# An encoder layer with 64 routed experts: experts' columns in units of 32 with groups of one size, and experts' weights laid out in runs of 16 KB and 8 KB a partition

## The reference, cut to what matters

```
scores = sigmoid(x @ w_router);  the 6 best of 64 experts a token (in 4 of 8 groups)
w = scores[chosen] / sum * 2.5
h_e = silu(x @ w_e_gate[e]) * (x @ w_e_up[e])      # 1024 -> 256
y   = sum over chosen e of w * (h_e @ w_e_down[e]) # 256 -> 1024
x   = LN(alpha * x + y + shared_expert(x))
```

## Time and profile before

| | |
|---|---|
| median of 3 runs | 1903.97 us (1901.08 to 1904.21) |
| the profiled execution's own time | 1900.44 us |
| its span | 1898.6 us |
| mean granted TensorE clock | 0.988 |
| PE busy | 1816.5 us, 96% |
| PE weight loads busy | 954.7 us, 50% |
| DVE / ACT / POOL busy | 655.2 / 322.4 / 148.0 us |
| DMA | 330.67 MB in 124958 packets, mean 174 GB/s |

### The profile page before, as it was taken

One profiled execution on the slowest core, in us unless ns is written; L12 is line 12 of the kernel. 1 busy time (PEld: TensorE's weight loads), 2 busy tenths in 40 slices (PEclk: granted clock), 3 DMA queues, 4 the chain that ended last, 5 costly groups with the idle time before them and its releaser, 6 DMA issues.

```text
span 1898.6 us, 18081 instructions
## 1 busy us (share of the span) xinstructions
PE 1816.5 (96%) x6817; PEld 954.7 (50%) x6817; DVE 655.2 (35%) x1008; ACT 322.4 (17%) x471; POOL 148.0 (8%) x159
## 2 busy tenths in 40 slices
PE   6999999999999999999999987999999999999976
PEld 3444456666666565556555544344444444444422
DVE  5011038888898863001115685000000000000019
ACT  1111121111111111111001210222222222222210
POOL 0000000000000000000000004111111111111112
PEclk9999999999999999999999999999999999999988
DMA  5115011110111001111162008999999999999547
GB/s 215 45 44 191 8 33 34 34 33 22 33 33 33 1 21 46 55 33 56 50 223 87 34 1 325 367 413 390 385 381 363 398 353 376 389 379 360 212 195 316
DMA packets 124958, 330.67 MB, mean 174 GB/s; under 512 B 11840, under 2 KB 68192, under 8 KB 106720
## 3 DMA queue, kind: packets, MB, share of 16 engines
q1 hardware_dynamic: 109200, 292.06, 40.9%
q0 software_dynamic: 15696, 37.77, 5.0%
HBM read 311.44 MB, written 37.75 MB: 184 GB/s over the span
## 4 chain that ended last, share of the span: by engine, by line
PE 87%; DVE 9%; DMA 1%; issue 1%; ACT 1%; DVEq 0%; SPq 0%; POOLq 0%; POOL 0%; ACTq 0%
PE pA L1020 19%; PE pg L667 10%; PE pB L1046 10%; PE pg L694 9%; PE pg L817 9%; PE pB L848 4%; PE pg L1007 3%; PE pB L895 2%; PE pA L895 2%; PE pA L840 2%; PE pg L707 2%; PE pB L750 2%; PE pX L908 1%; PE pA L787 1%; PE pA L750 1%
## 5 line engine op out<-in xcount | busy, mean ns | idle before, releaser
L694 PE MATMUL pg<-rA,hw 128*128 128x384 f32 x768 | 259.6, 486 | 0.7 <-ACT aTr L1154 0.7
L1735 DVE TENSOR_TENSOR rows<-rows,pA 128x256 f32<-128x256 f32 x53 | 22.3, 421 | 603.8 <-ACT rows L1266 603.8
L667 PE MATMUL pg<-rEF,rA 128*128 128x512 f32 x448 | 195.3, 598 | 3.1 <-ACT rCD L1133 3.1
L694 PEld LDWEIGHTS pg<-rA,hw 128*128 128x128 f32 x768 | 140.6, 190 | 84.1 <-ACT aTr L1154 0.9
L817 PE MATMUL pg<-rA,hw 128*128 128x384 f32 x512 | 165.3, 486 | 0.0
L1020 PE MATMUL pA<-rCD,aTr 128*64 128x512 f32 (+1 forms) x416 | 155.4, 594 | 0.0
L667 PEld LDWEIGHTS pg<-rEF,rA 128*128 128x128 f32 x448 | 85.8, 192 | 109.9 <-issue 109.9
L817 PEld LDWEIGHTS pg<-rA,hw 128*128 128x128 f32 x512 | 97.2, 190 | 67.6
L1020 PE MATMUL pA<-ew,aTr 128*64 128x512 f32 (+1 forms) x256 | 113.9, 598 | 0.0
L1020 PE MATMUL pA<-rEF,aTr 128*64 128x512 f32 (+1 forms) x256 | 113.2, 595 | 0.0
L1020 PE MATMUL pA<-rA,aTr 128*64 128x512 f32 (+1 forms) x240 | 106.8, 598 | 0.0
(11 more groups left out here) (304 smaller groups left out, 2387.3 us busy)
## 6 DMA issues: line engine op xcount, KB each, us to landing
rCD<-w_e_gate SPq DMA_DIRECT2D x22, 1024.0 KB, 8.7
rCD<-w_e_up SPq DMA_DIRECT2D x22, 1024.0 KB, 11.9
rCD<-w_e_down SPq DMA_DIRECT2D x22, 1024.0 KB, 12.8
hw<-w_in SPq DMA_DIRECT2D x40, 512.0 KB, 4.0
rA<-w_e_gate SPq DMA_DIRECT2D x11, 1024.0 KB, 5.4
rA<-w_e_up SPq DMA_DIRECT2D x11, 1024.0 KB, 7.5
rA<-w_e_down SPq DMA_DIRECT2D x11, 1024.0 KB, 12.5
ew<-w_e_gate SPq DMA_DIRECT2D x11, 1024.0 KB, 7.6
```

The lines of the kernel that those rows point to most:

```text
L667: last = mm(big_bank(fill), x1T[:, c, i * P:(i + 1) * P], strip[n % 2][:, c, :], start=(c == 0), stop=(c == KC - 1))
L694: last = mm(pg[:, n * 512:n * 512 + HALF], hw3[m][:, c, :], x1T[:, c, n * HALF:(n + 1) * HALF], start=(c == 0), stop=(c == KC - 1))
```

## The change

`rooms()` gives rank 0 one unit, ranks 1 to 10 four, ranks 11 to 42 three and the rest two: 179 units in place of 212, 45 rounds in place of 53, 46 blocks with the overflow's in place of 54. `pieces()` cuts all of a round in one size: 128 if one expert fills it, 64 if all borders are even, else 32, so that an expert with 96 columns in a round is three pieces of 32. Worked out from the code, the 45 rounds are 3 of one piece, 17 of two, 24 of four and a last one of three pieces of 32. On the host, gate and up are joined and laid out as (expert, 128 partitions, 4096 elements), one run of 16 KB a partition, and down as (expert, 128, 2048), one of 8 KB. SP issues two loads an expert in place of three. The layout in SBUF is the same.

```diff
 def rooms():
-    return [2] + [4] * 42 + [2] * 21
+    return [1] + [4] * 10 + [3] * 32 + [2] * 21

 def pieces(t):
-    out = []
+    spans = []
     for j in range(E):
         a = max(STARTS[j], t * UNITS) - t * UNITS
         z = min(STARTS[j + 1], (t + 1) * UNITS) - t * UNITS
-        while a < z:
-            n = 4 if a == 0 and z == 4 else 2 if a % 2 == 0 and z - a >= 2 else 1
-            out.append((j, a * UNIT, n * UNIT))
-            a += n
-    return out
+        if a < z:
+            spans.append((j, a, z))
+    whole = [z for _, _, z in spans] == [UNITS]
+    step = UNITS if whole else 2 if all(a % 2 == z % 2 == 0 for _, a, z in spans) else 1
+    return [(j, o * UNIT, step * UNIT) for j, a, z in spans for o in range(a, z, step)]
...
+        down_rows = [w[:, 4 * D:6 * D] for w in weights]
...
-            wg_d = d["w_e_gate"].rearrange("e (p c) n -> e p c n", c=KC)
-            wu_d = d["w_e_up"].rearrange("e (p c) n -> e p c n", c=KC)
-            wd_d = d["w_e_down"].rearrange("e (j p) n -> e p j n", p=P)
             def load_gate_up(e, n):
-                for m, src in ((0, wg_d), (1, wu_d)):
-                    sp.dma_start(slabs(gate_up[n][:, m * 2 * D:(m + 1) * 2 * D], KC),
-                                 src[bass.ds(e, 1), :, :, :].rearrange("e p c n -> (e p) c n")).then_inc(s_wgu[n], 16)
+                sp.dma_start(gate_up[n], d["w_e_gate_up"][bass.ds(e, 1), :, :].rearrange("e p n -> (e p) n")).then_inc(s_wgu[n], 16)
             def load_down(e, n):
-                sp.dma_start(wd[n], wd_d[bass.ds(e, 1), :, :, :].rearrange("e p j n -> (e p) j n")).then_inc(s_wd[n], 16)
+                sp.dma_start(down_rows[n], d["w_e_down"][bass.ds(e, 1), :, :].rearrange("e p n -> (e p) n")).then_inc(s_wd[n], 16)
...
-                    pe.wait_ge(s_wgu[j % NB], 32 * (j // NB + 1))
+                    pe.wait_ge(s_wgu[j % NB], 16 * (j // NB + 1))
...
-                pe.wait_ge(s_wgu[more], r * 32 + 32 * (used + 1))
+                pe.wait_ge(s_wgu[more], r * 16 + 16 * (used + 1))
...
+    gate, up, down = (arrays.pop(name) for name in ("w_e_gate", "w_e_up", "w_e_down"))
+    arrays["w_e_gate_up"] = np.concatenate([w.reshape(E, P, KC * F) for w in (gate, up)], axis=2)
+    arrays["w_e_down"] = np.ascontiguousarray(down.reshape(E, 2, P, D).transpose(0, 2, 1, 3)).reshape(E, P, 2 * D)
```

## The result

The changed kernel takes 1839.91 us (median of 4 runs, 1839.25 to 1843.92) against 1904.09 for the kernel before on the same chip: a ratio of 0.9669, 95% interval 0.965 to 0.9688, 64 us less. I forecast 1827 in a range of 1808 to 1855. A second set gave 1842.20 against 1903.75, ratio 0.968 (0.9667 to 0.9693). The profiled execution is the slowest of the first four, 1843.92 with a span of 1841.7; before it was 1900.44 and 1898.6.

What follows compares the result with a forecast made beforehand. DMA was to bound the expert stage: weights landing at 8.5 + 526.5 - 6.5 = 528.5 us plus 14 gave 542.5 against 619.7, 77 less; minus 2.5 for the first gather, net 75. Forecast 1827 us, range 1808 to 1855.

Steps and rivals of the forecast that it cites:

- PE's floor: Expert rounds: least time PE needs for the 45 rounds with fill and drain, 533 us.
- the price of a quad: Rounds of four 32-column pieces: 0.1 us a round over a pair, 2.4 us in all.
- The upper bound of 0.016 us a step: Quad rounds: issuing four load and matmul pairs takes at most 0.445 us against 0.43, 9 us in all.
- The rival in which groups of 32 take turns: Quad rounds: every step lasts 0.86 us in place of 0.43, 248 us more on PE, 2061; chance 0.05.
- the layout: Weight loads: larger blocks save 4.6 us on down and 2 on gate and up, together 6.5 us.
- The rival of a lower sustained rate: Expert stage: DMA sustains only 384 GB/s, so the gain is 35 us and the kernel takes 1866; chance 0.12.
- slow 16 KB blocks: Gate and up loads: 0.76 us a packet costs 64 us of DMA, 1891, or up to 2065; chance 0.03.
- the step from the bytes to the last weights' landing: Expert stage: 218.5 MB at 415 GB/s, 526.5 us, plus 8.5, less 6.5, land 528.5 us after the first up.
- 542.5: Expert stage, first up to end: last landing at 528.5 us plus 14 behind it, against 619.7 before.
- the clock at nothing: PE after DMA stalls: three or four might cost 1.7 us each, which DMA makes up; priced at nothing.
- the first gather: Start of the rounds: the gather stands behind larger preload blocks, 2.5 us later; later gathers hide.
- The rivals' 1816, 1866 and 2061: Whole-kernel times if PE stays the bound (chance 0.16), DMA sustains less (0.12), or groups take turns (0.05).

Runs made afterwards that it cites:

- the reordered kernels: Changed kernel with experts of 64 columns moved to the order's end: five 1832.75 us, eight 1827.40, eight with gathers first 1826.68, eight with 8 KB gate/up blocks 1832.37.
- f1: Changed kernel with SP waiting for the first two gathers to land before preloading the fifth and sixth expert: 1839.64 us, 0.9664 of the kernel before.
- e1: Changed kernel with its new rooms and pieces but the old weight layout (8 and 4 KB runs, three loads an expert): 1845.46 us, 0.9698 of the kernel before.
- e2: Kernel before with only the new weight layout (16 and 8 KB runs), old rooms and 53 rounds: 1904.98 us, 1.0013 of the kernel before.

## Why the prediction was right or wrong

**Right: the direction, the range and the bound.** DMA became the bound, at a mean share of 1.01 for 350 us. Landings take over 20 us. PE's floor was 533 us in the prediction; 532.3 was measured once DMA was lightened. The waits came in the later rounds, 17.0 us for my 5 to 15.

**Right: the price of a quad.** I took 0.1 us a round; it is none (7.00 for 7.02). The upper bound of 0.016 us a step from the rate of the transposes didn't bind: steps come 0.43 us apart, eight instructions in each. The rival in which groups of 32 take turns is out. The Trainium skill's some 4 ns per further tile ("TensorE: Matmul & The Clock Gate", Part 3) agrees with this trace in that a step's pieces start within 0.02 us; the 8 ns a step that the prediction made of it for a stream of steps don't show, 16 steps taking 7.00 us for 7.02.

**Right: the DMA rate and HBM.** I took 415 GB/s and 6.5 us for the layout, in effect 420; it was 423 from 1250 to 1500 us and 419 from the first free home (1209.4) to round 40. The rival of a lower sustained rate is out, and so are slow 16 KB blocks. The HBM limit of about 358 GB/s a core which the Trainium skill names ("DMA: Bandwidth & Descriptors", Specifications), there half of a stack's 716 for its two cores, doesn't bind in this program on one core: 423 over 250 us.

**Wrong: the step from the bytes to the last weights' landing, 528.5 us.** It divides the bytes by the engines' mean rate, as if sixteen engines were one. For their mean it came out: the sixteen landings of the last routed expert's down load lie 530.3 us after the first `up` in the mean. But the last of them comes at 543.0. The same lag of the last engine decides the wait that binds, at round 40: mean 476.7, last 490.8. Behind it lie 66 us of PE's work (1691.85 to 1757.69), since the last homes come free at round 40 and PE waits for nothing more. By the mean landing the sum is 476.7 + 65.8 = 542.5, which is the forecast; the 14 us by which the last engine lags behind the mean are what it missed. That is worked out and not run: no kernel here evens out the engines.

I also let the full queue last to the end, and followed the last load, 14 us before the end. PE never waits for that load: its `down` starts at 1754.06, 10 us after the last landing. With six homes the sum should go to round 40 and add the compute behind it; the reordered kernels show that this compute counts. Taken alone it changes nothing in the sum here, as the 542.5 shows.

**Wrong in part: the clock at nothing.** I wrote that DMA would make up what a slower PE loses. The price of 1.7 us for a stall, from the earlier trace rows, was near: 1.8, 2.2 and 3.0. The first two lie ahead of a later wait for weights, and there f1 speaks for me: 8 us won by PE ahead of the waits were lost again in them. The third lies behind the last wait and is paid in full. In the second profile the same `up` takes 8.36 in place of 10.02 us, 1.7 less, and the stage is 1.6 us shorter.

**Mis-sized: the first gather.** 2.5 us for the first, nothing for the second. It was 1.3 and, through the second, 4.0 in all. I followed one transfer where two stood in the same queue. I also read the 7.26 us of the earlier trace rows as PE's wait; they are the transfer, and PE sat idle for 10.38 (first fence above).

**The layout** was priced at 6.5 us; it gives 8.1 in the stage and takes 4 at the start: 3 to 6 us net, by the ratios of e1 and the two sets of the changed kernel, whose intervals touch or overlap e1's. That it gives nothing with 53 rounds, as the view of a stage without waits says, e2 confirms.

In all, 77 us of stage were 62.9, as 7.5 more of waits and 7 of clock; the start took 4.0 for 2.5. The forecast lay 13 us too low, at 75 of gain for 64. The rivals' 1816, 1866 and 2061 are counted from the profiled execution and not from the median, some 3.5 us too low, which changes no verdict.

## What to carry to other kernels

When fewer rounds make weight streaming the bound, sum it up to the last load that compute waits for, take the landing of the last DMA engine and not of their mean, and add the compute behind that point in full; then choose an order that leaves little compute behind the last freed buffers. A faster start or a cheaper block only pays where its engine is the bound: the same layout lost 2.5 us in one kernel and won an estimated 3 to 6 in the other. And where a large preload is queued, look at every small transfer that is issued behind it, not only at the first.

## What the runs showed of the hardware

Four column groups of 32, of two experts' moving operands in float32, run side by side at no cost over two of 64 (7.00 and 7.02 us for 16 steps). Blocks of 16 KB give a full queue 423 GB/s with the 4 KB rows of gathers and scatters among them, against 415 for 8 and 4 KB, but the first two gathers behind them hold PE 4 us longer. With a full queue the sixteen landings of a load drift apart, to 18.5 us (e1) and 27.6 us (the changed kernel) in the mean, against 3 to 5 in the kernels without waits for weights. After a wait of PE of 3.4 us its granted clock fell, and the next 7 us of matmuls took 1.8 longer; after waits of 1.4 us it stayed at 1.00.
